# Attention worked in pairs of maps: another order of scores, value products, transposes and copies, with the transposes in two pairs of banks

## The chip, the cores and the metric

The kernel runs on one core of one Trainium2 chip. The metric is the device time of one execution in microseconds (us), lower is better. Engines are named as in the profile: PE is TensorE's matrix product, PEld its weight load, DVE is VectorE, ACT is ScalarE, POOL is GpSimd, SP is SyncE.

## The reference, cut to what matters

Two trunk layers run over 640 tokens: 512 latent tokens on a grid of 8 rows of 64, and 128 context tokens. One layer is a projection, attention, an output projection, and a feed-forward of 16 retrieved experts in each of 8 heads. Only attention is touched here. It has three groups of heads, all of width 64 in their values:

```python
s = q @ k.T * scale                      # A: 6 heads, plus a bias and a window mask on latent keys
p = softmax(s)                           # C: 6 heads; latent queries read 512 latent + 128 context keys
o = p @ v                                # context queries read the 128 context keys only
# B: 4 heads of two maps each, mixed before the product with the values
pd = p[:, :, 0] - lam * p[:, :, 1]
ob = einsum('bhqs,bshd->bqhd', pd, v)
```

The kernel works with 128 queries at a time: four tiles of latent queries, whose maps are 128x640, and one tile of context queries, whose maps are 128x128. The text calls them wide and narrow.

## The kernel before, in words

`attention_plan` (L92) lists the work of a layer. A **map** is one softmax map of one head and one query tile. An **item** is one head and one query tile: one map in A and C, two maps in B. A **unit** is two heads of one query tile, whose outputs share a chunk of 128 rows of `oT`. The order is A, B, C; within a group the chunks (3, 2, 3); within a chunk the query tiles t = 0 to 4, t = 4 being the narrow one; within a tile the two heads. That is 100 maps, 80 items and 40 units a layer. Two neighbouring maps 2k and 2k+1 make a **pair**: in A and C a pair is a unit, in B a pair is one item and a unit is two pairs. A chunk of A or C has five pairs, a chunk of B ten.

All engines run programs of their own and meet at semaphores; the order on each is the order of its loop `for n in range(NMAP + LAG_V)`, with LAG_T = 3 and LAG_V = 4.

- **Scores.** At even n, PE writes the scores of maps n and n+1 (L540, L543, L545) into `pair[0]` and `pair[1]`, two pairs of PSUM banks. It waits before that until both exponentials of the pair before are done (`exp_done`, L532).
- **Maximum.** DVE adds the bias (A, wide, L1077) and takes the row maximum (L1078) of each map.
- **Exponential.** ACT computes it with the row sum as a by-product (L766) into one of eight `prob` buffers.
- **Scaling.** DVE inverts the row sum (L1083), POOL multiplies the map by it (L1337; in B only the second map, with -lambda), and in B DVE adds the two maps (L1089, `mixed`).
- **Transpose.** At step n, PE transposes the item whose last map is n-3 (L575), five blocks of 128 if wide and one if narrow, always into `pair[2]`. It waits for `scaled` or `mixed`, and until ACT has copied the item before out of `pair[2]` (L572).
- **Copy.** ACT copies the item of n-3 to `probT` (L776), right behind the exponential of map n.
- **Value products.** At step n, before the transpose, PE multiplies the unit whose last map is n-4 with the values (L560), ten products if wide, into bank 6 or 7 in turn; ACT copies the 128x128 result to `oT` (L781).

So PE's order in A and C is: scores of pair k; transpose of the second item of pair k-2; value products of pair k-2; transpose of the first item of pair k-1; scores of pair k+1. ACT's is: exponential, copy, exponential, copy and copy of the output.

Before the first maximum DVE computes the largest value (L1056 to L1066), for which PE makes one small product (`spread_sum`, L435). Behind attention PE waits for the last `oT` and goes on with the output projection. The weight blocks of that projection come through SP's queue and do not depend on the order inside attention.

Of the kernel before, what the change touches and what calls it, by code (L numbers as in the profile page):

```python
# [26 lines left out]
ALU = mybir.AluOpType  # L27
ACT = mybir.ActivationFunctionType
AX_X = mybir.AxisListType.X

P = 128
# [35 lines left out]
NRES = KC  # L67
OPAIR = (2, 1)
NPROB = 8
LAG_T, LAG_V = 3, 4  # L70
# [45 lines left out]

MAPS, ITEMS, UNITS = attention_plan()
NMAP, NITEM, NUNIT = len(MAPS), len(ITEMS), len(UNITS)
BY_LAST = {it["last"]: i for i, it in enumerate(ITEMS)}
UNIT_BY_LAST = {ITEMS[u["last"]]["last"]: i for i, u in enumerate(UNITS)}  # L120

SCALED = {m: i for i, m in enumerate([m for m, x in enumerate(MAPS) if x["kind"] != "B" or x["c"] == 1])}
MIXED = {i: n for n, i in enumerate([i for i, x in enumerate(ITEMS) if x["kind"] == "B"])}
# [43 lines left out]
def build(nc, a):  # L167
    with ExitStack() as ctx:
# [233 lines left out]
        def _(pe):  # L402
# [120 lines left out]
            def attention(l):  # L523
                pe.wait_ge(proj_evac, PROJ * l + NWIN)
                pe.wait_ge(post_fin, POSTS * (l + 1))
                pe.wait_ge(layer_in, 16 * 3 * (l + 1))
                for n in range(NMAP + LAG_V):
                    if n == 2:
                        spread_sum()
                    if n < NMAP and n % 2 == 0:  # L530
                        if n >= 2:
                            pe.wait_ge(exp_done, NMAP * l + n)  # L532
                        two = [(MAPS[n + x], pair[x]) for x in range(2)]
                        last = [None, None]
                        for lat in range(2 if MAPS[n]["t"] < TT - 1 else 1):
                            for x, (m, ps) in enumerate(two):
                                kp, kn, t = m["kp"], m["kn"], m["t"]
                                q = qk[kp:kp + kn, m["q"], t * P:(t + 1) * P]
                                if t == TT - 1:
                                    last[x] = pe.matmul(ps[:, 0:NCTX], q, qk[kp:kp + kn, m["k"], NLAT:TOK],  # L540
                                                        start=True, stop=True)
                                elif lat == 0:
                                    pe.matmul(ps[:, 0:NLAT], q, qk[kp:kp + kn, m["k"], 0:NLAT], start=True, stop=True)  # L543
                                else:
                                    last[x] = pe.matmul(ps[:, NLAT:TOK], q, kc[kp:kp + kn, m["cc"], :], start=True,  # L545
                                                        stop=True)
                        for x in range(2):
                            last[x].then_inc(score_done, 1)
                    if n - LAG_V in UNIT_BY_LAST:
                        u = UNIT_BY_LAST[n - LAG_V]  # L550
                        it = ITEMS[UNITS[u]["last"]]
                        pe.wait_ge(pt_done, NITEM * l + UNITS[u]["last"] + 1)
                        if u >= 2:
                            pe.wait_ge(o_evac, NUNIT * l + u - 1)
                        nb = TT if it["t"] < TT - 1 else 1
                        for b in range(nb):
                            for hh in range(2):
                                vs = slice(it["vcol"] - 64 + 64 * hh, it["vcol"] + 64 * hh)
                                v = vN[:, TT - 1 if nb == 1 else b, vs] if b < TT - 1 else vc[:, vs]
                                last = pe.matmul(psum[64 * hh:64 * hh + 64, 6 + u % 2, 0:P], v,  # L560
                                                 probT[:, u % 2, hh, b * P:(b + 1) * P],
                                                 start=(b == 0), stop=(b == nb - 1))
                        last.then_inc(pv_done, 1)
                    if n - LAG_T in BY_LAST:
                        i = BY_LAST[n - LAG_T]
                        it = ITEMS[i]
                        if it["kind"] == "B":
                            pe.wait_ge(mixed, NMIXED * l + MIXED[i] + 1)
                        else:
                            pe.wait_ge(scaled, NSCALED * l + SCALED[n - LAG_T] + 1)  # L570
# [114 lines left out]
        def _(act):  # L685
# [70 lines left out]
                        root(l, 1 + i - 5)  # L756

            def attention(l):
                for n in range(NMAP + LAG_V):
                    if n < NMAP:  # L760
                        m = MAPS[n]
                        w = TOK if m["t"] < TT - 1 else NCTX
                        act.wait_ge(max_done, NMAP * l + n + 1)
                        if n >= NPROB:
                            act.wait_ge(tr_done, NITEM * l + MAPS[n - NPROB]["item"] + 1)
                        act.activation(prob[:, n % NPROB, 0:w], pair[n % 2][:, 0:w], ACT.Exp,  # L766
                                       bias=stat[:, 0, n % NPROB:n % NPROB + 1],
                                       accum_out=stat[:, 1, n % NPROB:n % NPROB + 1]).then_inc(exp_done, 1)
                    if n - LAG_T in BY_LAST:
                        i = BY_LAST[n - LAG_T]  # L770
                        w = TOK if ITEMS[i]["t"] < TT - 1 else NCTX
                        act.wait_ge(tr_done, NITEM * l + i + 1)
                        u, hh = ITEMS[i]["unit"], ITEMS[i]["hh"]
                        if u >= 2:
                            act.wait_ge(pv_done, NUNIT * l + u - 1)
                        act.activation(probT[:, u % 2, hh, 0:w], pair[2][:, 0:w], ACT.Copy).then_inc(pt_done, 1)  # L776
                    if n - LAG_V in UNIT_BY_LAST:
                        u = UNIT_BY_LAST[n - LAG_V]
                        act.wait_ge(pv_done, NUNIT * l + u + 1)
                        tok = slice(UNITS[u]["t"] * P, (UNITS[u]["t"] + 1) * P)  # L780
                        act.activation(oT[:, UNITS[u]["chunk"], tok], psum[:, 6 + u % 2, 0:P],  # L781
                                       ACT.Copy).then_inc(o_evac, 1)
                act.wait_ge(o_evac, NUNIT * (l + 1))
                for b in range(2):
                    act.activation(sq[:, b, :], oT[:, 3 + b, :], ACT.Square).then_inc(b_sq, 1)
# [100 lines left out]
        def _(dve):  # L886
# [166 lines left out]
            def attention(l):  # L1053
# [14 lines left out]
                for n in range(NMAP + 2):  # L1068
                    if n < NMAP:
# [8 lines left out]
                        dve.tensor_reduce(stat[:, 0, n % NPROB:n % NPROB + 1], ps[:, 0:TOK if lat else NCTX], AX_X, ALU.max,  # L1078
                                          negate=True).then_inc(max_done, 1)
                    if 1 <= n <= NMAP:  # L1080
                        s = (n - 1) % NPROB
                        dve.wait_ge(exp_done, NMAP * l + n)
                        dve.reciprocal(stat[:, 2, s:s + 1], stat[:, 1, s:s + 1]).then_inc(rinv_done, 1)  # L1083
                    if n - 2 in BY_LAST and ITEMS[BY_LAST[n - 2]]["kind"] == "B":
                        it = ITEMS[BY_LAST[n - 2]]
                        w = TOK if it["t"] < TT - 1 else NCTX
                        s0, s1 = it["first"] % NPROB, it["last"] % NPROB
                        dve.wait_ge(scaled, NSCALED * l + SCALED[n - 2] + 1)
                        dve.scalar_tensor_tensor(prob[:, s0, 0:w], prob[:, s0, 0:w], stat[:, 2, s0:s0 + 1],  # L1089
                                                 prob[:, s1, 0:w], ALU.mult, ALU.add).then_inc(mixed, 1)  # L1090
                prologue(segment(SPLIT["wout", l, 0]))

                for n, c in enumerate(OCHUNKS):
# [359 lines left out]
```

## Time and profile before

| | us |
|---|---|
| median of 3 runs (5086.49 to 5101.38) | 5093.09 |
| the profiled execution's own time | 5102.09 |
| its span, first to last instruction | 5100.3 |
| PE busy in the span | 3820.1 (75%) |
| DVE busy | 2829.5 (55%) |
| ACT busy | 1444.8 (28%) |
| POOL busy | 1398.6 (27%) |
| mean granted clock of PE | 0.924 |

Busy time is the sum over the span, in which stages with different limits lie one behind the other. A granted clock of 1.00 is 2.4 GHz, 0.50 is 1.2 GHz. Attention of the first layer begins with the scores at 327.94 us and ends with the last copy to `oT`, which ends at 641.70 us; the second layer's begins at 2833.30 us.

### The profile page before, as it was taken

The numbers are of one execution on the slowest core, as the hardware profiler recorded it, in microseconds if no ns is written. First come the engines' busy times: TensorE is split into PE (matmuls) and PEld (weight loads), VectorE is DVE, ScalarE is ACT, GpSimd is POOL, SyncE is SP. The second block draws the span as 40 slices with busy tenths as digits, with TensorE's granted clock in tenths as the row PEclk, the third lists the DMA queues.
The fourth block names the chain that finished last, engine by engine and source line by source line (L and its number), as shares of the span: only waits on it lengthen the run. The fifth ranks groups of instructions, "written<-read, shape, count | busy, mean of one in ns | idle before, by whom it ended". The sixth has DMA issues, their size and how long they took to land.

```text
span 5100.3 us, 42883 instructions
## 1 busy us (share of the span) xinstructions
PE 3820.1 (75%) x14332; PEld 1753.3 (34%) x14332; DVE 2829.5 (55%) x6023; ACT 1444.8 (28%) x4223; POOL 1398.6 (27%) x1477
## 2 busy tenths in 40 slices
PE   7787779887777777777767776867777777777776
PEld 1364436222222222323234544432222222222222
DVE  2443365665675766745455334556657567575444
ACT  1224422222223222222222334222222222322222
POOL 1001200233343333433320111003333334333332
PEclk9886779999999999999988758989999999999999
DMA  7210012999999999999951000119999999999997
GB/s 253 72 40 1 1 54 73 389 407 406 417 414 416 416 406 413 401 416 401 418 188 50 15 1 17 63 68 410 412 412 416 411 419 406 420 416 395 406 419 290
DMA packets 214077, 1460.21 MB, mean 286 GB/s; under 512 B 23968, under 2 KB 24224, under 8 KB 49248
## 3 DMA queue, kind: packets, MB, share of 16 engines
q0 software_dynamic: 186496, 1355.11, 65.1%
q1 hardware_dynamic: 27360, 102.37, 5.9%
q8 instruction: 113, 1.85, 0.1%
q14 instruction: 108, 0.88, 0.0%
HBM read 1453.19 MB, written 4.19 MB: 286 GB/s over the span
## 4 chain that ended last, share of the span: by engine, by line
PE 41%; DMA 37%; DVE 12%; ACT 6%; issue 4%; SPq 0%; POOL 0%; ACTq 0%; DVEq 0%; POOLq 0%
DMA work<-expert_dram,work 29%; PE psum L656 17%; PE psum L448 10%; DMA hT<-expert_dram,work 7%; DVE work L1243 4%; PE psum L543 3%; PE psum L560 2%; PE psum L460 2%; PE psum L575 2%; ACT work L863 2%; PE psum L515 2%; DVE work L983 1%; ACT work L853 1%; ACT work L776 1%; PE psum L485 1%
## 5 line engine op out<-in xcount | busy, mean ns | idle before, releaser
L656 PE MATMUL psum<-work 128*128 128x512 f32 x3416 | 1606.1, 614 | 535.2 <-ACT work L863 535.2
L1243 DVE SCALAR_TENSOR_TENSOR work<-work,psum 128x1024 f32<-128x1024 f32 x854 | 1041.2, 1220 | 866.8 <-DMA work<-expert_dram,work 856.5
L1301 POOL DMA_INDIRECT work<-expert_dram,work x854 | 823.5, 964 | 1506.2 <-PE psum L656 1334.7
L656 PEld LDWEIGHTS psum<-work 128*128 128x128 f32 x3416 | 626.4, 193 | 1502.7 <-ACT work L863 866.5
L656 PE MATMUL psum<-hT,work 128*128 128x512 f32 x1704 | 810.1, 619 | 329.0 <-ACT work L863 329.0
L853 ACT ACTIVATE work<-work,xinv 128x2 f32<-128x2 f32 x640 | 189.1, 295 | 2390.5 <-DVE work L1243 1573.5
L1243 DVE SCALAR_TENSOR_TENSOR hT<-hT,psum 128x1024 f32<-128x1024 f32 x426 | 519.5, 1220 | 448.4 <-DMA hT<-expert_dram,work 448.1
L1301 POOL DMA_INDIRECT hT<-expert_dram,work x426 | 418.2, 982 | 864.0 <-PE psum L656 693.7
L656 PEld LDWEIGHTS psum<-hT,work 128*128 128x128 f32 x1704 | 315.0, 194 | 815.9 <-ACT work L863 496.3
L448 PE MATMUL psum<-hT,split 128*128 128x128 f16 (+1 forms) x2880 | 430.9, 310 | 58.0 <-DVE hT L1018 58.0
L863 ACT ACTIVATE work<-const,work 128x128 f32<-128x128 f32 x1280 | 434.1, 386 | 0.0
L448 PEld LDWEIGHTS psum<-hT,split 128*128 128x128 f16 x2880 | 230.8, 100 | 261.7 <-issue 62.5
L857 ACT ACTIVATE work<-work 128x1 f32<-128x1 f32 x1280 | 307.1, 287 | 20.7
L1078 DVE TENSOR_REDUCE stat<-psum 128x1 f32<-128x640 f32 (+1 forms) x200 | 141.0, 710 | 266.4 <-PE psum L545 209.0
L936 DVE SCALAR_TENSOR_TENSOR split<-ring,bscale,split 128x1024 f16<-128x1024 f32 x88 | 112.8, 1282 | 197.9 <-ACT split L697 197.3
L560 PE MATMUL psum<-work 128*64 128x128 f32 x1344 | 122.8, 342 | 122.8 <-ACT work L776 122.8
L766 ACT ACTIVATE work<-psum,stat 128x640 f32<-128x640 f32 (+1 forms) x200 | 141.7, 708 | 239.3 <-DVE stat L1078 238.6
L460 PE MATMUL psum<-ring,cT 128*2 128x512 f32 x384 | 179.6, 613 | 24.5 <-DMA ring<-w_mod_dram 24.5
L543 PE MATMUL psum<-work 64*128 64x512 f32 (+1 forms) x320 | 142.5, 982 | 50.3 <-ACT work L766 47.9
L1337 POOL TENSOR_SCALAR work<-work,stat 128x640 f32<-128x640 f32 (+1 forms) x120 | 85.2, 713 | 284.3 <-DVE stat L1083 284.3
L575 PE MATMUL psum<-const,work 128*128 128x128 f32 x672 | 141.5, 349 | 8.2 <-ACT work L776 8.2
L560 PEld LDWEIGHTS psum<-work 128*64 128x64 f32 x1344 | 97.2, 173 | 145.2 <-ACT work L776 145.2
(152 smaller groups left out, 2771.3 us busy)
## 6 DMA issues: line engine op xcount, KB each, us to landing
ring<-w_mod_dram SPq DMA_DIRECT2D x96, 512.0 KB, 4.9
ring<-w_in_dram SPq DMA_DIRECT2D x40, 512.0 KB, 3.6
ring<-w_query_dram SPq DMA_DIRECT2D x32, 512.0 KB, 3.5
work<-expert_dram,work POOLq DMA_INDIRECT x854, 8.5
ring<-w_out_dram SPq DMA_DIRECT2D x16, 512.0 KB, 3.6
hT<-expert_dram,work POOLq DMA_INDIRECT x426, 8.5
work<-rpb_dram POOLq DMA_DIRECT2D x4, 1344.0 KB, 19.7
xT<-xT_dram SPq DMA_DIRECT2D x1, 2560.0 KB, 11.5
```

Source lines behind the costliest of these rows:

```text
L448: last = pe.matmul(out[:, lo:hi_], w[:, i, k, :], x[:, j, k, lo:hi_], start=(s == 0 and n == 0), stop=(s == KC - 1 and n == 2))
L460: last = pe.matmul(psum[0:2, 2 + c % 2, :], cT[:, 2 * q + k, :], w[:, 512 * k:512 * k + 512], start=(q == 0 and k == 0), stop=(q == 3 and ...
L543: pe.matmul(ps[:, 0:NLAT], q, qk[kp:kp + kn, m["k"], 0:NLAT], start=True, stop=True)
L560: last = pe.matmul(psum[64 * hh:64 * hh + 64, 6 + u % 2, 0:P], v, probT[:, u % 2, hh, b * P:(b + 1) * P], start=(b == 0), stop=(b == nb - 1))
L575: last = pe.transpose(pair[2][:, b * P:(b + 1) * P], src[:, b * P:(b + 1) * P], con("ident"))
L656: last = pe.matmul(out[:, cols_], diag[:, n % NDIAG, :], rows[n % NBUF][:, D + 512 * half:D + 512 * half + 512], start=(s == 0), stop=(s = ...
L766: act.activation(prob[:, n % NPROB, 0:w], pair[n % 2][:, 0:w], ACT.Exp, bias=stat[:, 0, n % NPROB:n % NPROB + 1], accum_out=stat[:, 1, n % ...
L853: act.activation(act_out[:, s:s + 2], act_in[:, s:s + 2], ACT.Gelu_apprx_tanh, scale=xinv[:]).then_inc(gelu_done, 1)
L857: act.activation(coef[:, s + k:s + k + 1], act_out[:, s + k:s + k + 1], ACT.Copy, scale=weight[:, t % 2, s + k:s + k + 1]).then_inc(coef_d ...
L863: act.activation(diag[:, (n + k) % NDIAG, :], con("ident"), ACT.Copy, scale=coef[:, s + k:s + k + 1]).then_inc(diag_done, 1)
L1243: dve.scalar_tensor_tensor(u, u, 1.0, pair[t % 2], ALU.mult, ALU.mult, accum_out=act_in[:, s:s + 1]).then_inc(dot_done, 1)
L1301: pool.indirect_dma_start(rows[n % NBUF], None, a[f"expert{l}"], bass.IndirectOffsetOnAxis(expert[:, t % 2, s:s + 1], 0)).then_inc(row_in[ ...
```

## The change

PE, ACT and DVE each run a loop over pairs, `for k in range(NPAIR + 2)` (DVE over NPAIR), in place of the loop over maps with lags.

- PE at step k: scores of pair k; value products of the unit that ends with pair k-2; then all transposes of the items that end in pair k-1 (two in A and C, one in B), the first head's into `pair[2]` and the second head's into `pair[3]` (banks 6 and 7).
- The value products' output moves from banks 6 and 7 in turn to one place in bank 7, columns 256 to 383. They wait until the unit before is copied out, and a transpose of a second head waits until the output of the unit of this step is copied out, as that lies in its bank.
- ACT at step k: the output copy of the unit of pair k-2 first; then, for the two places x = 0, 1: the copy of item x of pair k-1 (if there is one), then the exponential of map 2k+x.
- DVE at step k: both maxima, then both reciprocals, then in B the mix of the same pair (before: one reciprocal behind each maximum, one map late, and the mix two maps late).
- `spread_sum` goes behind the scores of the first pair, as before. POOL and SP are untouched. The number of instructions of each kind is the same.

The helpers added are `pair_items(k)`, the items whose last map is in pair k, and `pair_unit(k)`, the unit that ends with pair k.

```diff
 # PE
-                for n in range(NMAP + LAG_V):
-                    if n < NMAP and n % 2 == 0:
-                        if n >= 2:
+                for k in range(NPAIR + 2):
+                    n = 2 * k
+                    if k < NPAIR:
+                        if k > 0:
                             pe.wait_ge(exp_done, NMAP * l + n)
...
-                    if n - LAG_V in UNIT_BY_LAST:
-                        u = UNIT_BY_LAST[n - LAG_V]
+                    u = pair_unit(k - 2)
+                    if u is not None:
                         it = ITEMS[UNITS[u]["last"]]
                         pe.wait_ge(pt_done, NITEM * l + UNITS[u]["last"] + 1)
-                        if u >= 2:
-                            pe.wait_ge(o_evac, NUNIT * l + u - 1)
+                        if u >= 1:
+                            pe.wait_ge(o_evac, NUNIT * l + u)
...
-                                last = pe.matmul(psum[64 * hh:64 * hh + 64, 6 + u % 2, 0:P], v,
+                                last = pe.matmul(psum[64 * hh:64 * hh + 64, 7, 2 * P:3 * P], v,
...
-                    if n - LAG_T in BY_LAST:
-                        i = BY_LAST[n - LAG_T]
+                    for i in pair_items(k - 1):
...
-                        if i > 0:
-                            pe.wait_ge(pt_done, NITEM * l + i)
+                        if i > 1:
+                            pe.wait_ge(pt_done, NITEM * l + i - 1)
+                        if it["hh"] == 1 and u is not None:
+                            pe.wait_ge(o_evac, NUNIT * l + u + 1)
                         src = prob[:, it["first"] % NPROB, :]
                         for b in range(TT if it["t"] < TT - 1 else 1):
-                            last = pe.transpose(pair[2][:, b * P:(b + 1) * P], src[:, b * P:(b + 1) * P], con("ident"))
+                            last = pe.transpose(pair[2 + it["hh"]][:, b * P:(b + 1) * P], src[:, b * P:(b + 1) * P],
+                                                con("ident"))
 # ACT, the new loop
+                for k in range(NPAIR + 2):
+                    u = pair_unit(k - 2)
+                    if u is not None:
                         act.wait_ge(pv_done, NUNIT * l + u + 1)
...
+                    turned = pair_items(k - 1)
+                    for x in range(2):
+                        if x < len(turned):
+                            i = turned[x]
...
+                            act.wait_ge(tr_done, NITEM * l + i + 1)
...
+                            act.activation(probT[:, it["unit"] % 2, it["hh"], 0:w], pair[2 + it["hh"]][:, 0:w],
+                                           ACT.Copy).then_inc(pt_done, 1)
+                        if k < NPAIR:
+                            n = 2 * k + x
...
+                            act.wait_ge(max_done, NMAP * l + n + 1)
...
+                            act.activation(prob[:, n % NPROB, 0:w], pair[x][:, 0:w], ACT.Exp,
...
 # DVE, the new loop
+                for k in range(NPAIR):
+                    for n in (2 * k, 2 * k + 1):
...
+                        dve.tensor_reduce(stat[:, 0, n % NPROB:n % NPROB + 1], ps[:, 0:TOK if lat else NCTX], AX_X,
+                                          ALU.max, negate=True).then_inc(max_done, 1)
+                    for n in (2 * k, 2 * k + 1):
+                        s = n % NPROB
+                        dve.wait_ge(exp_done, NMAP * l + n + 1)
                         dve.reciprocal(stat[:, 2, s:s + 1], stat[:, 1, s:s + 1]).then_inc(rinv_done, 1)
+                    for i in pair_items(k):
...
+                            dve.scalar_tensor_tensor(prob[:, s0, 0:w], prob[:, s0, 0:w], stat[:, 2, s0:s0 + 1],
+                                                     prob[:, s1, 0:w], ALU.mult, ALU.add).then_inc(mixed, 1)
```

## Rows read from the trace of the kernel before

**Rows 1.** The page, the chain that ended last, shares by line.
```profile
DMA work<-expert_dram,work 29%; PE psum L656 17%; PE psum L448 10%; DMA hT<-expert_dram,work 7%; DVE work L1243 4%; PE psum L543 3%; PE psum L560 2%; PE psum L460 2%; PE psum L575 2%; ACT work L863 2%; PE psum L515 2%; DVE work L983 1%; ACT work L853 1%; ACT work L776 1%; PE psum L485 1%
```

**Rows 2.** The page, forty slices: granted TensorE clock, in tenths.
```profile
PEclk9886779999999999999988758989999999999999
```

**Rows 3.** Windows by chunk: length, busy PE, PEld, DVE, ACT, POOL, clock, DMA, GB/s.
```profile
368.29:402.54 34.25, 23.42 (x163) 15.58 (x162) 13.04 (x28) 14.25 (x35) 7.10 (x10) 0.80 0.00 1
...
494.45:552.24 57.79, 42.53 (x200) 26.54 (x198) 23.04 (x50) 21.57 (x55) 7.88 (x10) 0.50 0.00 1
...
579.97:607.12 27.15, 18.99 (x163) 12.91 (x162) 7.82 (x20) 13.92 (x35) 7.10 (x10) 0.94 0.00 1
...
607.12:641.70 34.58, 23.63 (x194) 15.90 (x193) 9.11 (x22) 16.49 (x42) 7.47 (x11) 0.88 0.00 1
```

**Rows 4.** Timeline, C, wide pair: start, length, engine, line, idle before.
```profile
596.99 1.13 PE L543 MATMUL psum<-work 64*128 64x512 f32 x4
...
598.27 0.77 PE L575 MATMUL psum<-const,work 128*128 128x128 f32 x5
...
598.37 0.82 DVE L1078 TENSOR_REDUCE stat<-psum 128x1 f32<-128x640 f32 x1 [3.77 <-PE psum L545]
...
599.23 0.79 ACT L766 ACTIVATE work<-psum,stat 128x640 f32<-128x640 f32 x1 [1.26 <-DVE stat L1078]
...
600.01 0.69 ACT L776 ACTIVATE work<-psum 128x640 f32<-128x640 f32 x1
...
600.60 0.79 ACT L766 ACTIVATE work<-psum,stat 128x640 f32<-128x640 f32 x1
...
600.76 1.31 PE L560 MATMUL psum<-work 128*64 128x128 f32 x20 [1.72 <-ACT work L776]
...
602.00 0.77 PE L575 MATMUL psum<-const,work 128*128 128x128 f32 x5
...
602.70 0.49 PE L540 MATMUL psum<-work 64*128 64x128 f32 x4
...
602.80 0.70 ACT L776 ACTIVATE work<-psum 128x640 f32<-128x640 f32 x1 [1.32 <-PE psum L575]
```

**Rows 5.** Timeline, A, wide pair: the bias and the value products.
```profile
369.67 0.70 DVE L1077 TENSOR_TENSOR psum<-psum,work 128x512 f32<-128x512 f32 x1 [4.28 <-PE psum L545]
...
372.79 1.31 PE L560 MATMUL psum<-work 128*64 128x128 f32 x20 [2.46 <-ACT work L776]
```

**Rows 6.** Timeline, B, wide pairs.
```profile
515.62 2.40 PE L560 MATMUL psum<-work 128*64 128x128 f32 x20 [1.16 <-ACT work L776]
...
517.95 2.08 PE L543 MATMUL psum<-work 32*128 32x512 f32 x4
...
520.49 0.82 DVE L1078 TENSOR_REDUCE stat<-psum 128x1 f32<-128x640 f32 x1 [4.47 <-PE psum L545]
...
522.71 0.79 ACT L766 ACTIVATE work<-psum,stat 128x640 f32<-128x640 f32 x1
...
523.65 2.08 PE L543 MATMUL psum<-work 32*128 32x512 f32 x4 [1.94 <-ACT work L766]
```

**Rows 7.** Timeline, A: a transpose and its copy at the lower clock.
```profile
388.14 1.33 PE L575 MATMUL psum<-const,work 128*128 128x128 f32 x5
...
389.51 0.70 ACT L776 ACTIVATE work<-psum 128x640 f32<-128x640 f32 x1 [1.95 <-PE psum L575]
```

**Rows 8.** Timeline, B: GpSimd's scaling and VectorE's mix.
```profile
503.25 0.87 POOL L1337 TENSOR_SCALAR work<-work,stat,nlam 128x640 f32<-128x640 f32 x1 [4.83 <-DVE stat L1083]
...
504.16 0.88 DVE L1089 SCALAR_TENSOR_TENSOR work<-work,stat 128x640 f32<-128x640 f32 x1
```

**Rows 9.** Timeline, C: a narrow transpose, the last narrow pair.
```profile
612.13 0.33 PE L575 MATMUL psum<-const,work 128*128 128x128 f32 x1
...
629.77 0.49 PE L540 MATMUL psum<-work 64*128 64x128 f32 x4
...
630.64 0.37 ACT L766 ACTIVATE work<-psum,stat 128x128 f32<-128x128 f32 x1
```

More of the change, by code:

```diff
@@ L69 @@
 NPROB = 8
-LAG_T, LAG_V = 3, 4
 CONSTS = [("ident", 128), ("ones", 128), ("pairsum", 128), ("rotB", 128), ("rotC", 128),
@@ L118, with pair_items, pair_unit @@
 NMAP, NITEM, NUNIT = len(MAPS), len(ITEMS), len(UNITS)
+NPAIR = NMAP // 2
 BY_LAST = {it["last"]: i for i, it in enumerate(ITEMS)}
 UNIT_BY_LAST = {ITEMS[u["last"]]["last"]: i for i, u in enumerate(UNITS)}
+def pair_items(k):
+    return [BY_LAST[n] for n in (2 * k, 2 * k + 1) if n in BY_LAST] if 0 <= k < NPAIR else []
+def pair_unit(k):
+    return UNIT_BY_LAST.get(2 * k + 1) if 0 <= k < NPAIR else None
 SCALED = {m: i for i, m in enumerate([m for m, x in enumerate(MAPS) if x["kind"] != "B" or x["c"] == 1])}
@@ L548, in attention @@
                             last[x].then_inc(score_done, 1)
-                    if n - LAG_V in UNIT_BY_LAST:
-                        u = UNIT_BY_LAST[n - LAG_V]
+                    if k == 0:
+                        spread_sum()
+                    u = pair_unit(k - 2)
+                    if u is not None:
                         it = ITEMS[UNITS[u]["last"]]
                         pe.wait_ge(pt_done, NITEM * l + UNITS[u]["last"] + 1)
-                        if u >= 2:
-                            pe.wait_ge(o_evac, NUNIT * l + u - 1)
+                        if u >= 1:
+                            pe.wait_ge(o_evac, NUNIT * l + u)
                         nb = TT if it["t"] < TT - 1 else 1
@@ L758, in attention @@
             def attention(l):
[L759 to L778, printed above, removed]
@@ L779, in attention @@
+                for k in range(NPAIR + 2):
+                    u = pair_unit(k - 2)
+                    if u is not None:
                         act.wait_ge(pv_done, NUNIT * l + u + 1)
                         tok = slice(UNITS[u]["t"] * P, (UNITS[u]["t"] + 1) * P)
-                        act.activation(oT[:, UNITS[u]["chunk"], tok], psum[:, 6 + u % 2, 0:P],
+                        act.activation(oT[:, UNITS[u]["chunk"], tok], psum[:, 7, 2 * P:3 * P],
                                        ACT.Copy).then_inc(o_evac, 1)
+                    turned = pair_items(k - 1)
+                    for x in range(2):
+                        if x < len(turned):
+                            i = turned[x]
+                            it = ITEMS[i]
+                            w = TOK if it["t"] < TT - 1 else NCTX
+                            act.wait_ge(tr_done, NITEM * l + i + 1)
+                            if it["unit"] >= 2:
+                                act.wait_ge(pv_done, NUNIT * l + it["unit"] - 1)
+                            act.activation(probT[:, it["unit"] % 2, it["hh"], 0:w], pair[2 + it["hh"]][:, 0:w],
+                                           ACT.Copy).then_inc(pt_done, 1)
+                        if k < NPAIR:
+                            n = 2 * k + x
+                            w = TOK if MAPS[n]["t"] < TT - 1 else NCTX
+                            act.wait_ge(max_done, NMAP * l + n + 1)
+                            if n >= NPROB:
+                                act.wait_ge(tr_done, NITEM * l + MAPS[n - NPROB]["item"] + 1)
+                            act.activation(prob[:, n % NPROB, 0:w], pair[x][:, 0:w], ACT.Exp,
+                                           bias=stat[:, 0, n % NPROB:n % NPROB + 1],
+                                           accum_out=stat[:, 1, n % NPROB:n % NPROB + 1]).then_inc(exp_done, 1)
@@ L1067, in attention @@
                 dve.wait_ge(bias_ready, 6 * (l + 1))
-                for n in range(NMAP + 2):
-                    if n < NMAP:
+                for k in range(NPAIR):
+                    for n in (2 * k, 2 * k + 1):
                         m = MAPS[n]
@@ L1077, in attention @@
                             link(dve.tensor_tensor(ps[:, 0:NLAT], ps[:, 0:NLAT], b, ALU.add))
[L1078 to L1082, printed above, removed]
-                        dve.reciprocal(stat[:, 2, s:s + 1], stat[:, 1, s:s + 1]).then_inc(rinv_done, 1)
[L1084 to L1090, printed above, removed]
+                        dve.tensor_reduce(stat[:, 0, n % NPROB:n % NPROB + 1], ps[:, 0:TOK if lat else NCTX], AX_X,
[3 more added lines that the diff above has]
+                        dve.wait_ge(exp_done, NMAP * l + n + 1)
+                        dve.reciprocal(stat[:, 2, s:s + 1], stat[:, 1, s:s + 1]).then_inc(rinv_done, 1)
+                    for i in pair_items(k):
+                        it = ITEMS[i]
+                        if it["kind"] == "B":
+                            w = TOK if it["t"] < TT - 1 else NCTX
+                            s0, s1 = it["first"] % NPROB, it["last"] % NPROB
+                            dve.wait_ge(scaled, NSCALED * l + SCALED[it["last"]] + 1)
+                            dve.scalar_tensor_tensor(prob[:, s0, 0:w], prob[:, s0, 0:w], stat[:, 2, s0:s0 + 1],
+                                                     prob[:, s1, 0:w], ALU.mult, ALU.add).then_inc(mixed, 1)
                 prologue(segment(SPLIT["wout", l, 0]))
```

4 lines of the change are left out of this document (1 added, 3 removed).

## The prediction, as made before the changed kernel ran

> **What bounds the kernel now.** I read the chain of waits first: most of it is the experts' stage (its gathers, and the products of L656), and the lines of attention, L543, L560, L575 and L776, make up 8% together [rows 1]. The change touches nothing else, so this is a question of some 2 x 314 us: the first layer's attention runs from 327.94 to 641.70, and the second repeats it within 0.1 us pair by pair. Then I read the forty slices: the two deepest dips of PE's granted clock, slices 4 to 6 and 23 to 25, lie in the two attentions [rows 2]. The windows say how much: the mean granted clock is 0.80 in a chunk of A, 0.50 in all of a chunk of B, 0.94 and 0.88 in C, with no DMA to speak of [rows 3]. As the clock has two levels, 1.2 and 2.4 GHz, 0.80 is 40% of the time at the lower one; B is there all the time.
>
> No engine is full: in C's chunk PE is busy 19.0 of 27.15 us, ACT 13.9, DVE 7.8 [rows 3]. So it is a loop of waits, and the timeline gives it. In a wide pair of C, at the upper clock [rows 4]: scores of both maps 1.28 us (596.99 to 598.27), the maximum begins at 1.38, the first exponential 0.86 later, the copy of an older item 0.78 after that, and 0.75 after it the value products that waited for the copy; these take 1.24 (600.76 to 602.00), a transpose 0.70, and the next scores begin at 602.70. Sum: 1.38 + 0.86 + 0.78 + 0.75 + 1.24 + 0.70 = 5.71 us, the period. The second exponential lies beside the value products, and the other transpose beside the maximum: that is what the old order hides. A adds a bias of 0.70 ahead of the maximum [rows 5], some 6.4 us. PE rests once a period, 1.72 us in C and 2.46 in A [rows 4, 5].
>
> **The change, part by part.** Kinds and counts of instructions stay. What changes is which of them stand in the loop.
>
> PE now does scores(k), value products(k-2), both transposes of pair k-1. ACT does copy, exponential, copy, exponential in this order, strictly one behind the other. The first exponential of pair k thus waits behind the copy of an item that PE transposes after the scores of pair k *and* the value products. And the scores of pair k+1 wait for the second exponential. The loop becomes, upper clock: scores 1.28, products 1.24, first transpose to the start of its copy 0.80 (602.00 to 602.80), copy 0.59 (600.01 to 600.60), exponential 0.78, copy 0.59 [rows 4], and from the start of the second exponential to the next scores 0.94 (522.71 to 523.65) [rows 6]: 1.28 + 1.24 + 0.80 + 0.59 + 0.78 + 0.59 + 0.94 = **6.22 us**. The maximum (ready at 2.24, in A at 2.94) is hidden now under products and transpose, since the first exponential begins at 3.91. The second transpose (copy ready at 4.0) and the output copy lie beside other work too, and so does the wait of a second head's transpose for the output copy: that is done about 2.9, the transpose is due at 3.2. So C goes from 5.71 to 6.22, and A from 6.4 to 6.22: the bias goes off the path.
>
> At the lower clock the scores take 2.43 (maximum at 2.54 less the 0.10 seen above, 517.95 to 520.49), products 2.33 (515.62 to 517.95) [rows 6], transpose to copy 1.37 [rows 7]: 2.43 + 2.33 + 1.37 + 0.59 + 0.78 + 0.59 + 0.94 = **9.03**. The old loop there is 2.54 + 0.86 + 0.78 + 0.75 + 2.33 + 1.26 = 8.52 in C, and about 9.2 in A.
>
> A chunk of A or C has two such pairs; the other three touch the narrow tile. By the same steps, with a fifth of products and transposes (a narrow transpose 0.33, a narrow exponential 0.37 [rows 9]) I estimate 4.7, 5.0 (A 5.4) and 5.4 at the upper clock, 6.8, 7.4 and 7.4 at the lower. A chunk: C 27.5 or 39.7, A 27.9 or 39.7.
>
> How much of the time is at which clock? The trace of before doesn't show the new order, but near neighbours: PE's work in a pair is the same 3.9 us, and its rest in a period becomes 6.22 - 3.92 = 2.3 us, between A's 2.46 (40% low) and C's 1.72 (12 to 24% low, from 0.94 and 0.88) [rows 3 to 5]. Interpolated: 35%. Ends: 0% (a burst of one piece keeps the clock up) and 100% (as in B).
> - A chunk: 27.9 + 0.35 x 11.8 = 32.0 against 34.25, -2.2; two of them, -4.5. The first chunk, which begins with the wait for `spread_sum` and is mostly low already, I leave at 0 (between -5 and +2).
> - C chunk: 27.5 + 0.35 x 12.2 = 31.8 against 27.15, +4.6; two, +9.2.
> - The last chunk with its end is 34.58 us, 11.93 of it behind the last scores at 629.77 [rows 3, 9]. There the lags of three and four maps went one by one, with PE, ACT, PE in turn; now it is two steps. From the last scores I count 7.3 (upper) to 11.1 (lower), 8.6 at 35%, and 26.4 ahead of it: 35.0, +0.4.
>
> B is at the lower clock in every window, and PE will work less per us than now, so I keep it there. One item per pair, value products in every second. Pair without products: 2.43 + 1.37 + 0.59 + two exponentials without a copy between (0.88, estimated between 0.79 and 0.94) 0.88 + 0.94 = 6.21. With products: 2.33 more, 8.54. A wide unit 14.75. (POOL's scaling 0.87 and the mix 0.88 [rows 8] follow the second exponential and end about 2.1 after the next scores begin, under these scores' 2.43; DVE's next maximum queues behind the mix and is also covered until 2.5.) Three wide units, the first wide one behind a narrow (12.1) and the narrow one (9.6) make 3 x 14.75 + 21.7 = 66.0 against 57.79 [rows 3]: +8.2 a chunk, +16.4 a layer. At the upper clock the same count gives 50.2, -7.6 a chunk, and there the mix is what the transpose waits for.
>
> The second pair of banks removes a transpose's wait for the copy before it; in the steady loop the exponential between the copies covers that already, so it is worth something only at the end, counted above. The wait for `exp_done` on DVE (both reciprocals behind both maxima) holds only POOL, which has time.
>
> Sum per layer: -4.5 + 9.2 + 0.4 + 16.4 = +21.5; two layers +43. In general it is -0.1 + 62x us a layer, x the share of A and C at the lower clock.
>
> The row for the clock is this: in A, PE rests no longer than some 2.5 us at a time, and yet the clock is down 40% of the time. The Trainium skill (TensorE: Matmul & The Clock Gate, section "HAM oscillation — how this bites in real kernels") says the clock is lost where PE waits long between bursts, and advises to keep bursts in one piece; the waits it names are longer than any here. By it A and C would stay up, x = 0, and the sum would be B's alone, about nothing; by the row it is x = 0.35. I go by the row, since B and A already contradict the rule.
>
> **The rivals.**
> 1. *The clock stays up in A and C, B is low.* For it: one burst of 3.9 us per pair, a shorter rest than A's. Against: A's burst is of one piece already. x = 0: 0 us, or down to -10 with the first chunk: about 5098, no change.
> 2. *Faster: B comes up as well.* The denser burst lifts the clock in B, where scores of 2.43 become 1.28 and products 2.33 become 1.24. It decides from the point where B runs about two thirds of its time up (B's term 16.4 - 31.6y is zero at y = 0.52, and I want 15 us in all). Whole: 2 x (-0.1 - 15.2) = -31, 5071. Against: B's PE is busy 42.5 of 57.79 us at the low clock and hasn't risen once [rows 3]; it will be less busy.
> 3. *The clock falls for good in A and C.* The period is longer than C's, and the fall feeds itself: +124, 5226. For it: B. Against: A, whose low loop is as long as the new one, comes back up.
> 4. *The reordering doesn't reach the loop*, the copies being ready before they are asked for: would need a transpose before the products. Then 5.7 stays, no change.
>
> **How the numbers follow.** Forecast (x from 0.2 to 0.6) 0.63; rivals 0.14, 0.08, 0.11, 0.04. The sum is made against the profiled execution's 5102.09 (span 5100.3); that is 9 us above the median of 5093.09, so for a median I say 5093 + 43 = 5136. The likeliest case's own range is 5117 to 5167. The range for 8 in 10 takes in rival 1 and part of 3: 5083 to 5195. Faster or slower counts here from 0.3%, 15 us, about what can be told from no change with this kernel. Slower: 0.63 + 0.11, 0.74 in all. Same: rivals 1 and 4 less a little, 0.15. Faster: 0.11.
>
> **What would show it.** Right: in C the timeline has scores, products, transposes without a break, then PE rests over 2 us; the copy begins before the first exponential and waits for PE L575; scores wait for ACT L766 everywhere; periods of 6.2 or 9.0 in A and C, 6.2 and 8.5 in B; chunks of 66 in B. The idle time before the first exponential is put down to the transpose, not to the maximum. Wrong: granted clock in B above 0.6, or a C chunk under 28 us, or exponentials that start right behind the maximum.

## The result, and the profile after

The changed kernel takes 5132.96 us (median of 6, 5124.9 to 5146.63) against 5097.24 us (median of 6) for the kernel before: a ratio of 1.0079, 95% interval 1.0063 to 1.0095. It is slower by 36 us; 5136 was forecast, on a median before of 5093. The profiled execution has a span of 5140.0 us, 39.7 more than before.

The page, engines' busy time and granted clock: PE's busy time differs from before's 3820.1 by 8 us, and the clock's dips sit where they sat [rows 2].

```profile
PE 3828.2 (74%) x14332; PEld 1768.1 (34%) x14332; DVE 2841.9 (55%) x6023; ACT 1442.6 (28%) x4223; POOL 1399.0 (27%) x1477
...
PEclk9886689999999999999988857889999999999998
```

One attention now takes 337.6 us in the first layer (scores at 329.49, last output copied at 667.09) and 330.7 in the second (2855.41 to 3186.13), against 313.8 in each before: +23.8 and +16.9, 40.7 together. What lies outside differs by 1 us. The windows are those of [rows 3], with the third chunk of C and one chunk of A in the second layer added (columns as there: length, busy time of PE, PEld, DVE, ACT, POOL, granted clock, DMA share, GB/s):

```profile
367.36:401.38 34.02, 23.60 (x163) 16.51 (x163) 13.85 (x29) 14.00 (x35) 7.12 (x10) 0.75 0.00 1
...
500.56:565.15 64.59, 41.08 (x198) 25.83 (x198) 24.22 (x51) 21.48 (x55) 7.89 (x10) 0.55 0.00 1
...
597.73:631.08 33.35, 22.85 (x162) 15.84 (x162) 8.35 (x21) 13.88 (x35) 7.12 (x10) 0.80 0.00 1
...
631.08:667.09 36.01, 25.27 (x188) 18.47 (x188) 9.62 (x22) 14.97 (x39) 7.49 (x11) 0.81 0.00 1
...
2893.29:2924.14 30.85, 19.88 (x163) 14.21 (x163) 13.77 (x29) 14.03 (x35) 7.12 (x10) 0.89 0.00 1
```

A's chunk is 34.02 for 34.25, B's 64.59 for 57.79, C's second 33.35 for 27.15, and the last with its end 36.01 for 34.58. Busy times are much as before in B and DVE's and ACT's everywhere; PE's in C grows only as its clock is lower (0.80 for 0.94).

The timeline of a wide pair of C at the upper clock, which answers to [rows 4] (start, length, engine, line, idle before it and who ended that):

```profile
618.95 1.13 PE L550 MATMUL psum<-work 64*128 64x512 f32 x4 [2.39 <-ACT work L794]
...
620.23 1.31 PE L569 MATMUL psum<-work 128*64 128x128 f32 x20
...
620.33 1.55 DVE L1092 TENSOR_REDUCE stat<-psum 128x1 f32<-128x640 f32 x2 [1.24 <-PE psum L552]
...
621.47 1.31 PE L585 MATMUL psum<-const,work 128*128 128x128 f32 x10
...
621.59 0.28 ACT L775 ACTIVATE hT<-psum 128x128 f32<-128x128 f32 x1 [2.69 <-PE psum L569]
...
622.28 0.70 ACT L786 ACTIVATE work<-psum 128x640 f32<-128x640 f32 x1 [0.41 <-PE psum L585]
...
622.88 0.79 ACT L794 ACTIVATE work<-psum,stat 128x640 f32<-128x640 f32 x1
...
623.64 0.70 ACT L786 ACTIVATE work<-psum 128x640 f32<-128x640 f32 x1
...
624.23 0.80 ACT L794 ACTIVATE work<-psum,stat 128x640 f32<-128x640 f32 x1
...
625.18 0.80 PE L547 MATMUL psum<-work 64*128 64x128 f32 x4 [2.39 <-ACT work L794]
```

Read it as a loop: scores (618.95), value products (620.23), two transposes (621.47), the output copy, which ACT has awaited for 2.69 us (621.59), the first item's copy, which has waited another 0.41 us for PE L585 (622.28), exponential (622.88), copy (623.64), exponential (624.23), next scores (625.18), for which PE has been idle 2.39 us, until ACT L794. The maxima begin at 620.33, and the first exponential, which before started 0.86 us behind the first maximum, starts 2.55 behind it. The period is 6.23 us; 6.22 was worked out. At the lower clock it is 9.04 (9.03), in B 8.44 with value products (8.54) and 6.11 without (6.21). Before, the pair took 5.71 [rows 4].

Two pairs of B, one without and one with value products:

```profile
526.95 2.08 PE L550 MATMUL psum<-work 32*128 32x512 f32 x4 [2.35 <-ACT work L794]
...
528.10 0.88 DVE L1104 SCALAR_TENSOR_TENSOR work<-work,stat 128x640 f32<-128x640 f32 x1 [1.01 <-POOL work L1352]
...
530.75 0.70 ACT L786 ACTIVATE work<-psum 128x640 f32<-128x640 f32 x1 [3.85 <-PE psum L585]
...
531.35 0.79 ACT L794 ACTIVATE work<-psum,stat 128x640 f32<-128x640 f32 x1
...
532.12 0.79 ACT L794 ACTIVATE work<-psum,stat 128x640 f32<-128x640 f32 x1
...
533.06 2.08 PE L550 MATMUL psum<-work 32*128 32x512 f32 x4 [2.35 <-ACT work L794]
...
537.94 0.28 ACT L775 ACTIVATE hT<-psum 128x128 f32<-128x128 f32 x1 [4.93 <-PE psum L569]
...
539.19 0.70 ACT L786 ACTIVATE work<-psum 128x640 f32<-128x640 f32 x1 [0.97 <-PE psum L585]
```

The mix (L1104) is over 2.03 us behind the start of the scores, 526.95, before they end: so in these pairs VectorE's order costs nothing. ACT is idle for 3.85 us until PE L585 in the one, and for 4.93 until L569 and 0.97 until L585 in the other.

Who kept ACT waiting in the first layer's attention, before and after (waiter, whom it waited for: us in total, times, longest):

```profile
ACT work L766 <- DVE stat L1078: 119.3, 48, 7.4
...
ACT work L776 <- PE psum L575: 49.3, 39, 2.8
```

```profile
ACT hT L775 <- PE psum L569: 139.1, 40, 4.9
...
ACT work L786 <- PE psum L585: 60.9, 43, 3.9
...
ACT work L794 <- DVE stat L1092: 8.9, 6, 7.4
```

Before it was the maximum, ahead of the exponential. Now it is PE, ahead of the copies: what ACT could have begun (the exponential) stands behind them in its queue. The larger part, 139.1 us, is put down to the value products, as the output copy (L775) stands ahead of the items' copies; the transposes have 60.9 us.

### The profile page after: what moved, and what is told of

Read it like the earlier page. It is cut to its first block, busy times and chain, and to the rows that moved or that the text cites. A ratio compares the mean times of both kernels' runs of the same rounds, so it can differ in the third digit from the quotient of the medians.

```text
span 5140.0 us, 42883 instructions
## 1 busy us (share of the span) xinstructions
PE 3828.2 (74%) x14332; PEld 1768.1 (34%) x14332; DVE 2841.9 (55%) x6023; ACT 1442.6 (28%) x4223; POOL 1399.0 (27%) x1477
## 4 chain that ended last, share of the span: by engine, by line
PE 41%; DMA 37%; DVE 11%; ACT 7%; issue 4%; POOL 0%; SPq 0%; ACTq 0%; DVEq 0%; POOLq 0%
DMA work<-expert_dram,work 21%; PE psum L667 17%; DMA hT<-expert_dram,work 15%; PE psum L456 10%; DVE work L1258 3%; ACT work L794 3%; PE psum L550 3%; PE psum L569 2%; DVE hT L1258 2%; PE psum L585 2%; PE psum L468 2%; ACT work L877 2%; PE psum L523 2%; DVE work L997 1%; ACT work L867 1%
## 5 line engine op out<-in xcount | busy, mean ns | idle before, releaser
L1097 DVE RECIPROCAL stat<-stat 128x1 f32<-128x1 f32 x200 | 32.7, 163 | 271.3 <-ACT work L794 271.3
L794 ACT ACTIVATE work<-psum,stat 128x640 f32<-128x640 f32 (+1 forms) x200 | 140.9, 708 | 17.9 <-DVE stat L1092 17.9
L569 PE MATMUL psum<-work 128*64 128x128 f32 x1344 | 135.0, 367 | 2.8 <-ACT work L786 2.8
L585 PE MATMUL psum<-const,work 128*128 128x128 f32 x672 | 128.4, 342 | 11.5 <-DVE work L1104 9.3
```

The costliest lines, as they stand in the source:

```text
L569: last = pe.matmul(psum[64 * hh:64 * hh + 64, 7, 2 * P:3 * P], v, probT[:, u % 2, hh, b * P:(b + 1) * P], start=(b == 0), stop=(b == nb - 1))
L585: last = pe.transpose(pair[2 + it["hh"]][:, b * P:(b + 1) * P], src[:, b * P:(b + 1) * P], con("ident"))
L794: act.activation(prob[:, n % NPROB, 0:w], pair[x][:, 0:w], ACT.Exp, bias=stat[:, 0, n % NPROB:n % NPROB + 1], accum_out=stat[:, 1, n % NPR ...
```

## The experiments

Ratios are to the kernel before, run beside it on the same chip. The median of the kernel before lies between 5091 and 5097 us in the groups of runs, so small differences between two experiments are better read from the ratios than from the medians. The edits put one part of the change into the old kernel (e7, e8, e5), take one part out of the new one (e1, e9), double a suspected cost (e6), or follow the theory to a faster order (e2, e10, e11).

| run | us, median | ratio | 95% interval |
|---|---|---|---|
| the change | 5133.0 | 1.0079 | 1.0063 to 1.0095 |
| before, ACT's order alone (e7) | 5117.1 | 1.0061 | 1.0039 to 1.0082 |
| before, VectorE's order alone (e8) | 5092.2 | 0.9998 | 0.9985 to 1.0011 |
| before, the banks alone (e5) | 5091.4 | 1.0001 | 0.9982 to 1.0021 |
| the change, exponential before copy (e1) | 5028.6 | 0.9872 | 0.9848 to 0.9896 |
| the change, one pair of banks (e9) | 5171.9 | 1.0151 | 1.0128 to 1.0174 |
| the change, value products twice (e6) | 5185.6 | 1.0191 | 1.0172 to 1.0209 |
| both exponentials before both copies (e2) | 4976.5 | 0.9762 | 0.9732 to 0.9791 |
| the same with one pair of banks (e10) | 5052.7 | 0.9918 | 0.9892 to 0.9943 |
| e2, and A's scores split (e11) | 4954.2 | 0.9731 | 0.9703 to 0.9759 |

**e7, the kernel before with ACT's new order alone.**

```diff
 for n in range(NMAP + LAG_V):
+    copy of the item of n - LAG_T
     exponential of map n
-    copy of the item of n - LAG_T
```

> The kernel before with one edit: on ACT, at each step the copy comes first and the exponential second. Loop, PE order and banks stay the old ones. By my theory this order alone brings the price of the whole change in A and C: scores 1.28, transpose to copy 0.80, copy 0.60, value products 1.29, transpose to copy 0.80, copy 0.59, exponential to scores 0.94 = 6.3 us instead of 5.71 in C (upper clock), 9.7 instead of 8.5 (lower); in A 6.3 instead of 6.4; in B about nothing, since PE with its products is the longer leg there (12.9 a unit). 15 to 35 us slower in all, 5110 to 5135 us. Rivals (banks, or VectorE's order): no change, 5097.

5117 us, +26. A wide pair of C at the upper clock:

```profile
625.75 1.13 PE L543 MATMUL psum<-work 64*128 64x512 f32 x4 [1.57 <-ACT work L774]
...
627.12 0.82 DVE L1078 TENSOR_REDUCE stat<-psum 128x1 f32<-128x640 f32 x1 [2.74 <-PE psum L545]
...
627.83 0.70 ACT L767 ACTIVATE work<-psum 128x640 f32<-128x640 f32 x1 [1.97 <-PE psum L575]
...
628.43 0.79 ACT L774 ACTIVATE work<-psum,stat 128x640 f32<-128x640 f32 x1
...
630.63 0.70 ACT L767 ACTIVATE work<-psum 128x640 f32<-128x640 f32 x1 [1.32 <-PE psum L575]
...
631.23 0.79 ACT L774 ACTIVATE work<-psum,stat 128x640 f32<-128x640 f32 x1
...
632.16 1.13 PE L543 MATMUL psum<-work 64*128 64x512 f32 x4 [1.57 <-ACT work L774]
```

The exponential (628.43) starts 1.31 us behind the maximum's start (627.12) where it was 0.86, as it queues behind the copy of 627.83, and the second one (631.23) behind a copy that waits for the second transpose. The period is 6.41 us (625.75 to 632.16); I had summed 6.3. C's chunks go from 27.7 and 27.2 to 34.1 and 33.0 us, B's stay at 57.2 and 58.0, A's go *down* from 34.3 to 32.0 and 30.5. So this order in the old kernel hurts in C alone, at granted clocks of 0.72 and 0.79 there instead of 0.83 and 0.94. The change loses 28 of its 41 us in B, where e7 loses nothing: that its +0.61% is near the change's +0.79% is no proof for B. What holds there is seen in e1.

**e8 and e5, VectorE's order alone and the banks alone.**

```diff
 # e8, VectorE
-for n: maximum of n; reciprocal of n-1; mix of the item of n-2
+for k: maxima of 2k, 2k+1; reciprocals of 2k, 2k+1; mix of pair k
 # e5, PE and ACT
-transposes in pair[2]; outputs in bank 6 or 7 in turn
+transposes in pair[2 + hh]; outputs in psum[:, 7, 2 * P:3 * P]; waits as changed
```

> The kernel before with VectorE's part of the change alone: both maxima of a pair, then both reciprocals, then in B the mix of the same pair; PE, ACT and the banks are the old ones. My theory: VectorE is off the loop, and what it delays (the reciprocal of a first map waits behind the second maximum) ends at 3.0 us where the first exponential is done only at 3.1, so nothing moves: 5085 to 5102 us, a ratio of 1 within 0.3%. Rival (VectorE's new order, with the mix ahead of the next maximum, costs part of the 36 us): 5110 or more, the loss in B.

> The kernel before with the banks of the change alone: second heads' transposes and their copies in pair[3], value products always in bank 7, with the waits that these need; all orders are the old ones. My theory: no change in the loop, since the copy that a transpose waited for has ended under the scores (5085 to 5100 us; a few us may go at the end of each attention). Rival (the single output place and its wait cost part of the 36 us): 5105 or more.

Both 0 within about 0.2%. Neither part costs by itself in the median. In e5's profiled execution the chunks of A are longer all the same, 36.65 and 34.99 us in the first layer (granted clock 0.72 and 0.76) against 34.25 and 34.26 (0.80), and the second chunk of C in the second layer is shorter, 25.70 us (1.00) against 27.16 (0.94). PE's new order was not put into the old kernel by itself. (The reverse, the changed kernel with VectorE's old order, was not tried: the reciprocal of map 2k would wait for an exponential that waits for a copy, a transpose and a mix queued behind that reciprocal.)

**e1, the changed kernel with exponential before copy.**

```diff
 for x in range(2):
-    copy of item x of pair k-1
     exponential of map 2k+x
+    copy of item x of pair k-1
```

> The changed kernel with one edit: on ACT, for each of the two places, the exponential comes first and the copy second. My theory (the loop is lengthened because the first exponential queues behind a copy whose transpose stands behind scores and value products): the first exponential starts behind the maximum or the output copy (2.9 us after the scores begin at the upper clock, 5.1 at the lower), the copy still lies between the exponentials. A wide pair of C goes from 6.22 to 5.2 us (upper clock) and from 9.03 to 7.7 (lower); in A 5.3 and 7.7; a wide unit of B from 14.6 to about 13.4. About 40 us less per layer, 5050 to 5070 us, so below the kernel before (5097). Rival 1 (the single output place in bank 7 and its wait cost the time): no change, 5133. Rival 2 (VectorE's new order costs it): no change, 5133.

5028.6 us, 104 less than the change and 1.3% less than before; more than I expected. The wide pair of C:

```profile
570.98 1.13 PE L550 MATMUL psum<-work 64*128 64x512 f32 x4 [1.28 <-ACT work L785]
...
573.62 0.28 ACT L775 ACTIVATE hT<-psum 128x128 f32<-128x128 f32 x1 [2.10 <-PE psum L569]
...
573.80 0.79 ACT L785 ACTIVATE work<-psum,stat 128x640 f32<-128x640 f32 x1
...
574.57 0.70 ACT L795 ACTIVATE work<-psum 128x640 f32<-128x640 f32 x1
...
576.10 0.49 PE L547 MATMUL psum<-work 64*128 64x128 f32 x4 [1.28 <-ACT work L785]
```

The output copy (573.62) is now the first thing, and the exponential follows at 573.80, 2.82 us after the scores instead of 3.93; the period is 5.12 (570.98 to 576.10), at the lower clock 7.66. Both were worked out to within 0.1. What I had undervalued is most likely the narrow and mixed pairs and the clock: 1.00 over the second chunk of C in the first layer (0.86 in the second layer), 0.87 and 0.81 in A. In B, a pair without and one with value products, all at the lower clock:

```profile
496.38 2.08 PE L550 MATMUL psum<-work 32*128 32x512 f32 x4 [1.57 <-ACT work L785]
...
502.08 2.07 PE L550 MATMUL psum<-work 32*128 32x512 f32 x4 [1.94 <-ACT work L785]
...
509.74 2.08 PE L550 MATMUL psum<-work 32*128 32x512 f32 x4 [1.57 <-ACT work L785]
```

They take 5.70 and 7.66 us, 13.36 a unit, against 5.70 and 7.25 (12.95) before and 6.11 and 8.44 (14.55) in the change. So ACT's order makes 1.2 of the 1.6 us that a unit of B loses, and 0.4 stays. That this is PE's order, with the value products ahead of the transposes, is not shown: no run takes that order alone. On the whole the rest of the change is worth something, and ACT's order turned it into a loss.

**e6, every group of value products issued twice.**

```diff
+for again in range(2):
     for b in range(nb):
         for hh in range(2):
             last = pe.matmul(psum[64 * hh:64 * hh + 64, 7, 2 * P:3 * P], v, ...)
```

> The changed kernel with every group of value products issued twice (same operands, same place; the result is the same). By my theory the products stand in the loop between scores and transposes, so each wide pair of A and C grows by a full group, 1.24 us at the upper clock and 2.33 at the lower (6.22 to 7.5, 9.03 to 11.4), and B's pair with products from 8.44 to 10.8. 32 wide groups a layer: 50 to 65 us a layer more, 5230 to 5260 us, less what a busier PE gains in clock (then from 5190). If the products were hidden beside ACT and VectorE (rival: the bound is elsewhere, as in the maxima or the row sums), 5133 to 5145.

5185.6 us, +53 against the change: the products are in the loop, and a wide pair at the upper clock is 7.32 us instead of 6.23. That is 1.09 more, where I had worked out 1.24: the doubled group takes 2.34 us (40 products) and not 2.48. The time is also just under the 5190 that I had as the lower end. But even if every group had run at the upper clock, 64 wide groups at 1.10 us more would be 70 us, above the 53 (57 by the ratios). The clock gave the rest back, as the windows of A, B and C show:

```profile
363.27:400.00 36.73, 26.21 (x246) 20.27 (x247) 13.95 (x29) 13.91 (x35) 7.12 (x10) 0.86 0.00 1
...
503.74:572.55 68.81, 45.82 (x283) 31.92 (x283) 24.30 (x51) 21.48 (x55) 7.88 (x10) 0.63 0.00 1
...
604.89:639.51 34.62, 24.55 (x246) 19.56 (x246) 8.35 (x21) 13.90 (x35) 7.12 (x10) 0.90 0.00 1
```

0.86, 0.63 and 0.90 where the change has 0.75, 0.55 and 0.80 in the first layer.

**e2, both exponentials before both copies.**

```diff
-output copy; for x: copy x, exponential x
+exponential 0; output copy; exponential 1; copy 0; copy 1
```

> The changed kernel with ACT in the order: exponential, output copy, exponential, copy, copy. By my theory the copies leave the loop altogether: the next scores follow the second exponential, and PE's own work becomes the bound. A wide pair of C 4.2 us at the upper clock (the second exponential starts at 3.25, next scores 0.94 later) and 7.3 at the lower (all PE: 2.43 + 2.33 + 2 x 1.26); A 5.3 and 7.3 (two bias additions and two maxima on VectorE bind at the upper); a wide unit of B 11.3 (lower). PE without gaps should also hold the upper clock longer. 50 to 65 us less per layer than the changed kernel, 5000 to 5035 us. Rival 1 (the output bank) and rival 2 (VectorE's order): 5133, or a small part of this.

4976.5 us, 2.4% less than before and below what I expected. C:

```profile
540.66 1.13 PE L550 MATMUL psum<-work 64*128 64x512 f32 x4
...
542.90 0.79 ACT L780 ACTIVATE work<-psum,stat 128x640 f32<-128x640 f32 x1 [1.11 <-DVE stat L1093]
...
543.85 0.80 ACT L780 ACTIVATE work<-psum,stat 128x640 f32<-128x640 f32 x1
...
544.62 1.30 ACT L796 ACTIVATE work<-psum 128x640 f32<-128x640 f32 x2
...
544.78 1.13 PE L550 MATMUL psum<-work 64*128 64x512 f32 x4
```

The period is 4.12 us (540.66 to 544.78), in which PE works 3.9; scores wait for nothing that the row names. The copies (544.62, two in 1.30 us) lie under the next scores. A, where two biases and two maxima are on the path, takes 5.38 (5.3 worked out). B takes 5.10 and 5.98 for its two pairs at the lower clock (11.1 a unit; 11.3 worked out), and 4.52 for a pair without products at the upper one; its granted clock is 0.67 and 0.60 now.

**e9 and e10, one pair of banks, in the change and in e2.**

```diff
-if i > 1: pe.wait_ge(pt_done, NITEM * l + i - 1); transposes in pair[2 + hh]
+if i > 0: pe.wait_ge(pt_done, NITEM * l + i);     transposes in pair[2]
```

> The changed kernel with one pair of banks for all transposes, so that each waits for the copy before it; orders as changed. My theory: the first copy ends at 4.0 us of a wide pair (upper clock), the second transpose is ready for its copy at 4.8 instead of 4.0, where ACT asks for it at 4.7: +0.1 us a pair; at the lower clock 8.2 against 7.5, +0.7. So 5 to 10 us a layer more, 5140 to 5153 us. Rival (the second pair of banks is what the change lives on): 5180 or more.

> The kernel with both exponentials ahead of the copies (the earlier run of 4977 us) with one pair of banks for all transposes. My theory: here the second pair of banks counts, as the second transpose would wait for a copy that now comes behind both exponentials: a wide pair of C 5.4 us instead of 4.12, of A 6.6 instead of 5.38, B unchanged, 25 to 35 us a layer, 5025 to 5050 us. Rival (the banks never matter): 4977.

e10 came as worked out in C, 5.47 us for 4.12, and a little above in time (5053). e9 did not: 5172 is +39, where I had +7 to +20. Its wide pair is 6.48 us, +0.25:

```profile
592.53 0.79 ACT L792 ACTIVATE work<-psum,stat 128x640 f32<-128x640 f32 x1
...
592.78 0.74 PE L583 MATMUL psum<-const,work 128*128 128x128 f32 x5 [0.88 <-ACT work L784]
...
593.56 0.70 ACT L784 ACTIVATE work<-psum 128x640 f32<-128x640 f32 x1
```

The second transpose starts at 592.78, when the first copy has ended, and its copy starts at 593.56, 1.03 us behind the exponential instead of 0.76. I had 0.1 for this 0.25. Some 24 wide pairs of A and C a layer at 0.25 are 12 us in both; the larger part of what the trace shows is in A's chunks, 38.2 and 36.0 us in the second layer at clocks of 0.69 and 0.74 where the change has 30.9 and 30.8 at 0.89. But e9's profiled execution is only 20 us longer than that of the change (spans of 5160.2 and 5140.0), so the traces hold about half of the 39 us. The second pair of banks does help in the changed kernel, and by more than the 12 us of the wait; how much of the rest is the clock, these runs don't separate.

**e11, a version that beats both.** In A, each map's two score products go out together, and those of the first map wait only for the first exponential.

```diff
-pe.wait_ge(exp_done, NMAP * l + n)   # both maps, products interleaved
+for x in range(2):
+    pe.wait_ge(exp_done, NMAP * l + n - 1 + x)
+    scores of map n + x
```

> The kernel with both exponentials ahead of the copies, and in A the scores of the first map wait only for the first exponential of the pair before (each map's two products issued together instead of interleaved). In A its 5.38 us are scores, two biases, two maxima, the second exponential; the first map's part can start under the second exponential. My theory: 4.6 to 4.9 us a wide pair of A, 6 to 10 us a layer less, 4957 to 4967 us. Rival: the interleaved issue is what makes the four products of a pair take 1.28 us, and undoing it costs as much as the earlier start brings: 4977 or more.

4954.2 us, 2.7% less than before and 3 us under the range. The second chunk of A:

```profile
352.57:375.69 23.12, 19.57 (x163) 13.61 (x162) 13.57 (x28) 13.92 (x36) 7.16 (x11) 1.00 0.00 1
```

23.12 us where e2 has 27.25 (granted clock 0.87) and before had 34.25 (0.80), all at the upper clock, 1.00. Part of this is the clock: the third chunk runs at 0.87 as in e2 and takes 25.37 us, 1.9 less. A wide pair at the upper clock is 4.84 us.

## Why the prediction was right, step by step

- *The loop.* The seven terms of the new loop gave 6.22 and 9.03 us; 6.23 and 9.04 were measured. The maxima, the second transpose, the output copy and the mix are hidden as said. One sign was put wrongly: the idle time ahead of the first exponential is put down to the transpose for 0.41 us only, and for 2.69 us to the value products, since ACT's first task in a step is the output copy. The length of the loop does not change by it, as the transpose ends last.
- *Why it is longer.* The step was that the first exponential queues behind a copy that PE releases late. e7 puts this order alone into the old kernel, e1 takes it alone out of the new one: +0.61% and -2.07% of the time before. For C this is shown from both sides. For B, where most of the loss lies, only e1 shows it (1.2 of 1.6 us a unit), as e7's B doesn't move. The rivals banks (e5) and VectorE's order (e8) are 0 in the old kernel.
- *B, +16.4 a layer.* Measured +14.3 and +13.8 (65.10 and 64.59, 64.59 and 64.64 us a chunk against 66.0 forecast). The pairs are 0.1 shorter each than summed, and a few ran in part at the upper clock: the granted clock of the four chunks is 0.55 to 0.59. B was not at the lower clock in every window before, either: its first chunk had 0.55.
- *C, +9.2.* Measured +11.1 in each layer: chunks of 32.6 and 33.4 against 31.8. The loop was right, the share of the lower clock too small: 58% and 40%, not 35%.
- *A, -4.5 and 0 for the first chunk.* Measured -0.4 and -2.5 in the first layer, -6.9 and -2.5 in the second. *The end, +0.4:* +1.4.
- *The sum*, +43: +40.7 in the traces, +36 in the medians. That it is so near is partly luck: terms were off both ways, C up and A and B down, and A's alone differs by 6.5 us between the two layers of one execution.
- *The clock by neighbours' gaps.* 35% was a guess between rows; the measured shares in A and C go from 22 to 58%. That it would fall at all with rests of some 2.4 us was right. By the rule of the Trainium skill (TensorE: Matmul & The Clock Gate, "HAM oscillation — how this bites in real kernels") A and C would have stayed up; the windows above (0.75, 0.80) disagree, as those of before did. Its advice, to keep PE's bursts together, agrees with e2 and e11 in part: with rests nearly gone the second chunk of C (e2) and of A (e11) has 1.00 in both layers, but the first chunk of C in e2 has 0.81 and the third of A in e11 0.87.

The rivals: no clock loss in A and C (5098), all of B at the upper clock (5071), clock lost for good (5226) are all excluded by the windows; that the reordering doesn't reach the loop is excluded by the timeline.

## What to carry to other kernels

Ask of each instruction that is moved forward not what it costs but when its input is ready, and what stands behind it in its engine's program: here a 0.6 us copy moved ahead of a 0.8 us exponential made the exponential wait for three steps of PE. Write the loop out once, term by term, from one period of the timeline; it gave the periods of the change to 0.1 us and those of the experiments to 0.2, and it also names the better order (first what the bound engine waits for, then what only feeds buffers). A part that is worth nothing alone, as the second pair of banks in the old order, can be worth 1.6% in another order (e10 against e2).

## What the runs showed of the hardware that was not expected

- The same program runs the same chunk of A in 34.0 us in one layer and 30.8 in the other, in one execution, at granted clocks of 0.75 and 0.89. Where PE rests in every period, the clock's share can't be read off the order of the instructions: the second chunk of C has 1.00 and 0.86 in e1's two layers (rests of 1.28 us) and 0.94 and 1.00 in e5's (1.73 us). Where PE hardly rests (the second chunk of C in e2, of A in e11) it was 1.00 in both layers, but 0.87 in e11's third chunk of A.
- More work can be cheap where PE is idle enough to lose its clock: 64 wide and 16 narrow groups of value products cost 53 us in e6, less than the 70 us that the wide ones alone add at the upper clock.
